# Expert tiles of a two-block transformer: eight raw and six split places for weights instead of four and four

## What is computed

```python
def swiglu(h, wg, wu, wd):
    return (jax.nn.silu(h @ wg) * (h @ wu)) @ wd

def moe_swiglu(h, router, bias, wg, wu, wd):
    logits = (h @ router).astype(jnp.float32) + bias.astype(jnp.float32)
    top_logit, top_idx = lax.top_k(logits, TOP_K)
    ...
    out = jnp.zeros_like(h)
    for e in range(N_EXPERTS):
        out = out + gates[..., e:e + 1] * swiglu(h, wg[e], wu[e], wd[e])
    return out
```

## Time and profile before

| | us |
|---|---|
| median of three executions | 3074.38 (3071.87 to 3077.40) |
| the profiled execution | 3072.45 |
| its span, first to last instruction | 3070.6 |
| first tile of experts to the end | from 2346.4 to 3070.6 |
| of it, six whole tile periods | 2418.3 to 2806.7 |

### The profile page before, as it was taken

The page is one execution under the profiler, slowest core; times in us unless marked ns, Lnnn a source line. Parts: engine busy times, 40 slices in busy tenths (PEclk is TensorE's granted clock), DMA queues, the critical chain, the costliest instruction groups (busy, mean ns, idle before and its releaser), DMA issues.

```text
span 3070.6 us, 54310 instructions
## 1 busy us (share of the span) xinstructions
PE 2717.5 (88%) x21600; PEld 2488.4 (81%) x21600; DVE 2141.7 (70%) x3622; ACT 1384.3 (45%) x2027; POOL 122.4 (4%) x115
## 2 busy tenths in 40 slices
PE   7989899998998998898789998897989988988877
PEld 7878899897888997797779997786888766776655
DVE  6898677588876757674557666755566778777666
ACT  4444444444534444333344443332344565666554
POOL 0000000000000000000000000000000000001454
PEclk9999999999999999898899998997999999999999
DMA  5533445454444553212235542111434777787676
GB/s 193 171 128 133 145 160 193 136 179 153 136 145 138 190 176 108 72 71 70 96 104 175 191 159 96 56 57 63 143 113 146 251 262 251 267 280 264 214 235 209
DMA packets 153738, 485.88 MB, mean 158 GB/s; under 512 B 17136, under 2 KB 27760, under 8 KB 153232
## 3 DMA queue, kind: packets, MB, share of 16 engines
q1 hardware_dynamic: 135664, 424.68, 41.3%
q0 software_dynamic: 13584, 51.91, 5.1%
q10 hardware_dynamic: 4240, 5.81, 0.7%
HBM read 481.29 MB, written 1.05 MB: 157 GB/s over the span
## 4 chain that ended last, share of the span: by engine, by line
PE 56%; DVE 21%; DMA 10%; ACT 7%; issue 6%; POOL 0%; DVEq 0%; ACTq 0%; SPq 0%; POOLq 0%
PE ps L1762 15%; PE ps L1764 14%; PE ps L1763 14%; PE ps L1767 12%; DVE wl L2564 8%; ACT wh L2233 4%; DMA wf<-in_moe_down 3%; DVE b L2576 3%; DVE b L2568 3%; DMA wf<-in_moe_up_a 3%; DMA wf<-in_moe_up_a,b 2%; DVE SC L2576 2%; DVE SC L2568 1%; DMA wf<-in_moe_down,b 1%; DVE RS L2568 1%
## 5 line engine op out<-in xcount | busy, mean ns | idle before, releaser
L2564 DVE TENSOR_TENSOR wl<-wf,wh 128x1024 fp32r<-128x1024 f32 (+3 forms) x934 | 1081.8, 1187 | 354.4 <-ACT wh L2233 349.8
L2233 ACT ACTIVATE wh<-wf 128x1024 fp32r<-128x1024 f32 (+3 forms) x934 | 932.3, 1026 | 462.8 <-PE ps L1764 224.1
L1762 PE MATMUL ps<-b,wh 128*128 128x256 f32 x3096 | 900.5, 291 | 105.5 <-DVE wl L2564 62.2
L1763 PE MATMUL ps<-b,wh 128*128 128x256 f32 x3096 | 888.3, 287 | 0.0
L1764 PE MATMUL ps<-b,wl 128*128 128x256 f32 x3096 | 887.9, 287 | 0.0
L1762 PEld LDWEIGHTS ps<-b,wh 128*128 128x128 f32 x3096 | 607.0, 196 | 119.0 <-issue 88.0
L1763 PEld LDWEIGHTS ps<-b,wh 128*128 128x128 f32 x3096 | 606.9, 196 | 0.2
L1764 PEld LDWEIGHTS ps<-b,wl 128*128 128x128 f32 x3096 | 606.6, 196 | 0.0
L1762 PE MATMUL ps<-wh,b 128*128 128x512 f32 (+2 forms) x748 | 305.8, 409 | 92.6 <-DVE wl L2564 82.1
L1762 PE MATMUL ps<-HH,wh 128*128 128x256 f32 x1264 | 374.0, 296 | 12.7 <-DVE wl L2564 12.6
L1763 PE MATMUL ps<-HL,wh 128*128 128x256 f32 x1264 | 363.8, 288 | 0.0
(11 more groups left out here) (212 smaller groups left out, 2446.3 us busy)
## 6 DMA issues: line engine op xcount, KB each, us to landing
wf<-in_w_in_b SPq DMA_DIRECT2D x112, 512.0 KB, 4.3
wf<-in_moe_up_a SPq DMA_DIRECT2D x112, 512.0 KB, 4.6
wf<-in_w_in SPq DMA_DIRECT2D x80, 512.0 KB, 3.6
wf<-in_moe_down SPq DMA_DIRECT2D x77, 512.0 KB, 4.6
wf<-in_w_ffn_g SPq DMA_DIRECT2D x44, 512.0 KB, 3.6
wf<-in_w_ffn_u SPq DMA_DIRECT2D x44, 512.0 KB, 4.6
wf<-in_moe_up_b SPq DMA_DIRECT2D x56, 384.0 KB, 3.9
wf<-in_w_out SPq DMA_DIRECT2D x32, 512.0 KB, 3.5
```

The source lines that it names most:

```text
L1762: e.matmul(o, stat[0], mov[0], start=first, stop=False)
L1763: e.matmul(o, stat[0], mov[1], start=False, stop=False)
L2233: e.activation(u.whi, u.buf, ACT.Copy).then_inc(u.hi[0])
L2564: e.tensor_tensor(u.wlo, u.buf, u.whi.bitcast(F32), SUB).then_inc(u.lo[0])
```

## The change

Slots are now objects in a ring that can grow: each knows who used it last (`last`), and a unit waits for that instead of the unit four before. Before the first tile four raw slots are added in the arena at 14000 to 18095 (free once the last matmul of `first_up` has read `xg`), so that there are eight. After `add_x0` two pairs of split slots are added at 3584 to 7679 (free once `add_x0` has read `F0`), so that there are six. The tiles' steps split up to four units ahead (`AHEAD_TILE`), all others still two.

```diff
-    SLOT, NRAW, NSPL, AHEAD = 1024, 4, 4, 2
+    SLOT, NRAW, NSPL, AHEAD, AHEAD_TILE = 1024, 4, 4, 2, 4
...
+    class Slots:
+        def __init__(self, views):
+            self.slots, self.i = [], -1
+            self.more(views, None)
+
+        def more(self, views, after):
+            for v in views:
+                a = Step("slot")
+                a.v, a.last = v, after
+                self.slots.append(a)
+
+        def take(self):
+            self.i = (self.i + 1) % len(self.slots)
+            return self.i, self.slots[self.i]
+
+    def used_by(hi, lo, free):
+        a = Step("use")
+        a.hi, a.lo, a.free = hi, lo, free
+        return a
+
+    raws, splits = Slots(WF), Slots(list(zip(WH, WL)))
...
-        u.z, u.f = u.i % NSPL, u.i % NRAW
+        f, raw = raws.take()
+        _, split = splits.take()
+        u.raw_after, u.split_after, raw.last, split.last = raw.last, split.last, u, u
...
+                if read is not None:
+                    read[:] = [st.bk.full]
...
-            st.split_to = u.i + 1 + AHEAD
+            st.split_to = u.i + 1 + AHEAD_TILE
...
-        fd0 = yield from first_up(ins["moe_wg_2"], ins["moe_wu_2"], 11, F0, ADDED, routing)
+        x_read = []
+        fd0 = yield from first_up(ins["moe_wg_2"], ins["moe_wu_2"], 11, F0, ADDED, routing, x_read)
...
+        raws.more([big(14000 + SLOT * i, SLOT) for i in range(4)], used_by(x_read, None, None))
...
+                splits.more([[big(3584 + 2 * SLOT * i + SLOT * z, SLOT, dt=F32R) for z in range(2)] for i in range(2)], used_by(None, None, end0))
...
-                if u.i >= NSPL:
-                    E.wait_ge(units[u.i - NSPL].free)
+                if u.split_after is not None:
+                    E.wait_ge(u.split_after.free)
...
-                E.wait_ge(units[u.i - NRAW].hi)
-                E.wait_ge(units[u.i - NRAW].lo)
+                E.wait_ge(u.raw_after.hi)
+                E.wait_ge(u.raw_after.lo)
```

More of the change, by code:

```diff
@@ L288, in unit_of @@
         u.i = len(units)
-        u.z, u.f = u.i % NSPL, u.i % NRAW
         u.src, u.m, u.n, u.rows = src, m, n, rows
-        u.raw = P.next(f"w_raw{u.f}" if rows is None else f"w_rows{u.f}", 16)
+        f, raw = raws.take()
+        _, split = splits.take()
+        u.raw_after, u.split_after, raw.last, split.last = raw.last, split.last, u, u
+        u.raw = P.next(f"w_raw{f}" if rows is None else f"w_rows{f}", 16)
         u.hi = P.next("w_hi")
@@ L295, in unit_of @@
         w = u.m * u.n
-        u.buf, u.whi, u.wlo = WF[u.f][:, 0:w], WH[u.z][:, 0:w], WL[u.z][:, 0:w]
+        u.buf = raw.v[:, 0:w]
+        u.whi, u.wlo = [x[:, 0:w] for x in split.v]
         units.append(u)
@@ L963, in block1_mix, with first_up @@
         residual_rms(Y, yd, 0.5, ys)
-    def first_up(Wg, Wu, nt, F2, parts, side=None):
+    def first_up(Wg, Wu, nt, F2, parts, side=None, read=None):
         fd, late = {}, []
@@ L3311, in sp_program @@
                 continue
-            if u.i >= NRAW:
-                E.wait_ge(units[u.i - NRAW].hi)
-                E.wait_ge(units[u.i - NRAW].lo)
+            if u.raw_after is not None:
+                E.wait_ge(u.raw_after.hi)
+                E.wait_ge(u.raw_after.lo)
             e.dma_start(u.buf.rearrange("p (m n) -> p m n", n=u.n), u.src).then_inc(u.raw[0], 16)
```

## The result

The median fell from 3073.7 us (four executions) to **2955.3 us** (2950.21 to 2962.21), a ratio of 0.9615 with a 95% interval of 0.9592 to 0.9637. The span of the profiled execution is 2951.6 us, 119.0 less than before.

The account below looks back on a forecast made before the run. The prediction took a latency loop of too few raw slots as the bound. SP periods −49, start +5 and POOL tiles −39 summed to −83 us, giving 2991 us, with a range of 2958 to 3025.

Parts of the forecast that it names:

- The latency loop: Tiles: four raw slots, each reused after 6.8 to 7.3 us, bind; eight allow a unit per 0.9, even 1.3 us.
- 53.6 + 2 + 1 = 56.5 us: SP tile period: TensorE floor, later banks at the scatter, first matmuls starting behind a wait; six periods save 49 us.
- +8: Start: first new raw slot waits for the last first-expert gemm, so the third unit is ready 8 us later.
- +2: Start: new split slots wait for the first expert's last matmul behind the additions, costing 2 us.
- −3: Start: splitting four ahead covers part of VectorE's overflow work in the first tile, saving 3 us.
- −2: Start: the first tile's own waits for transfers go, saving 2 us.
- (35 − R) × 1.25 us: POOL tiles: least break time for loads with R low-part runs per 35 units; R = 16 gave 65 us a period.
- POOL is not held: Rival, POOL tiles: the 105 units also go at 1.61 us each, saving 64 us; 2966 us in all, chance 0.20.
- Long runs starve POOL: Rival, POOL tiles: ten low-part runs, 72 us a period, saving only 17 us; 3013 us in all, chance 0.20.
- rows 12: Earlier trace, POOL tiles: one load of 2.72 us ending 0.82 after four back-to-back low parts; read as loads being held.
- The wait moves to the banks: Rival: two extra splits cost more steps than the scatter; SP periods 60 us, 3021 us in all, chance 0.12.
- Slower: Rival: transfers at their limit at 268 GB/s, more slots only lengthen landings; +30 us, 3104 in all, chance 0.04.

Follow-up runs that it names:

- e1: Changed kernel with eight raw slots, but only four split places and two units ahead: 2971.1 us, 0.9685 of the kernel before.
- e2: Changed kernel with only four raw slots, keeping six split places and four units ahead: 3072.1 us, 1.0006 of the kernel before.
- e10: Changed kernel with eight raw slots and four units ahead, but without the two added split places: 2975.1 us, 0.9696.
- e5: Changed kernel with both rings beginning again at their first old place when they grow: 2939.3 us, 0.9579.
- e9: Kernel of e5 (old places first) with two more raw slots, ten in all: 2934.3 us, 0.9565.
- e7: Changed kernel with splits two instead of four units ahead in the three overflow tiles: 2955.7 us, 0.9633.
- e11: Kernel of e5 (old places first) with splits three units ahead in the overflow tiles: 2943.3 us, 0.9594.
- e6: Changed kernel with overflow tiles loading fixed experts' weights by SP's plain loads instead of POOL's indirect ones: 2943.2 us, 0.9595.
- e12: Changed kernel with the overflow tiles' low part made as raw unit times zero, one SBUF input instead of two: 2938.9 us, 0.9586.

## Why the prediction missed

The direction, the cause and the start were right; the size was 36 us short in the span, in two steps: 14 us in the SP periods and 20 in the POOL tiles (the rest, 2 us, lies ahead of the first tile).

**The latency loop: right.** Slots alone give 97 us, the rest alone nothing (e1, e2), and ScalarE's wait for transfers is gone. That 1.3 us a unit would be enough was borne out down to six slots.

**The SP period: mis-sized.** "53.6 + 2 + 1 = 56.5 us" measured 54.1, 14 us over six periods. The floor of TensorE was right to 0.5. The 2 us at the scatter are not there: the wait is 0.40 us, where it was 0.48. I let VectorE arrive late at the gate step. But its 49.8 us of work in 54.1 leave it ahead, so the two extra splits are done before TensorE ends the step and delay nothing. They cost a wait of 1.94 us when the places are missing (e10). The 1 us for starts behind a wait fell away with the waits: the period opened at 2585.10 has no other gap of TensorE over 0.1 us.

**The start: right.** "+8", "+2", "−3" and "−2" made +5, measured +5.5. The third unit starts 5.3 us later than before by the time of the span, 7 counted from the earlier gemm end, for the 8 expected. Behind the additions TensorE waits 2.1 and 1.0 us where it waited 3.6 once: −0.5 for "+2" and "−3". That leaves −1 for the "−2".

**The POOL tiles: the step that failed.** "A POOL load does not get through while low parts follow each other without a gap" was read from one load. VectorE and POOL of the changed kernel, in order of time:

```profile
2815.91 2.35 DVE L2597 TENSOR_TENSOR wl<-b,wh 128x1024 fp32r<-128x1024 f32 x2
2818.19 1.22 DVE L2597 TENSOR_TENSOR wl<-wf,wh 128x1024 fp32r<-128x1024 f32 x1
...
2817.11 1.97 POOL L3331 DMA_INDIRECT b<-in_moe_down,b  x1 [0.30 <-issue]
2819.39 0.94 POOL L3331 DMA_INDIRECT b<-in_moe_down,b  x1 [0.31 <-issue]
```

The low part under which the load starts ends at 2818.26 and the next begins at 2818.19, with no gap. The load ends at 2819.08, 0.82 us behind the first, while the second still runs. In the changed kernel 49 loads start under a low part that another follows within 0.06 us. Of them 46 are over within 0.95 us of the first one's end; three (2.3 to 2.7 us long) are held to the end of the next as well. So a run without gaps as a rule lets a load through every 1.97 + 0.30 = 2.27 us, not one in all. The load of the earlier trace rows was one of the exceptions, and the trace before had the rule: 21 of 24. Longer exceptions exist, 4.0 us in e5 and e9, 4.7 in e7, 7.9 in e11. What decides between the two cases no run here shows. Two groups of the line's loads (count, duration ns min/median/max):

```profile
L3331 POOL DMA_INDIRECT b<-in_moe_up_a,b x24: 933/946/2662, 2740.3 to 2897.8; - x24
...
L3331 POOL DMA_INDIRECT wf<-in_moe_down,b x17: 933/1054/1968, 2811.8 to 2928.4; - x17
```

With R runs the formula asked for (35 − R) × 1.25 us of breaks. The changed kernel has 13 and 19 runs in two overflow periods (12 and 14 when breaks under 0.06 us are not counted), for which it gives 68 and 61 us or more; both last 58. The forecast of 65 was 7 us a tile too long, 20 in all. The average load takes 1.26 us and 0.30 go between: 35 of them are **54.7 us**, just above TensorE's 54.1. Raw units come late, the gate step stands behind them, and TensorE waits 2.7 and 3.0 us for it; the stretch at half clock behind each wait makes up the 58 (e7). The forecast had no term for the clock, though it was 0.95 in these tiles before. e9 and e6 agree: more slots change nothing in sum, plain loads give 54.2.

**The rivals.** "POOL is not held" (2966; first in the list, though the working calls it the second) was nearest, though its mechanism is wrong: loads are held, but the queue costs some 10 us where I had priced the hold at 25. "Long runs starve POOL" fell with the reading of rows 12. "The wait moves to the banks" is true in the overflow tiles alone (2.7 us), and there it comes with late raw units. "Slower" fell: 319 GB/s over 270 us, though landings grew to 8.3 us at the longest, over the 7 I had named. The Trainium skill (SBUF — State Buffer, Who interferes with whom) infers that a tensor-tensor operation leaves descriptor writing alone, but has it contend with what GpSimd reads from SBUF when both its inputs lie there. The prediction took the first half alone. The loads here read their row numbers from SBUF and are held, 1.97 us in place of 0.94; that agrees with the second half, and which access is held no run shows. The time that the first half would have given (2966) was nearer than mine. The section also lists tensor-scalar among the operations that can take the shared ports; e12 agrees, with 1.33 us behind one of 0.69.

## What to carry to other kernels

When a wait for transfers shows in a chain that returns to the same buffer, divide that loop by the number of buffers and compare with the next bound; the smallest number that falls well under it is enough (here six where five were not). The average is not all: with five the loop gave 51 us a period and the late units still made TensorE wait. An added lead costs nothing while the engine that makes it arrives early, so compare its work with the period before pricing the delay. Where a wait of TensorE is taken away or made, look at the granted clock behind it: here waits of 1.9 to 3.2 us were most often followed by 3.4 us at half the clock, another 1.7 us. And a rule of contention read from a single instruction is worth checking on all its kind: a hundred loads were in the trace.

## What was not expected of the hardware

A POOL indirect load ends 0.82 us after the VectorE operation under which it starts, most often also if another follows at once (46 of 49 in the changed kernel): 1.97 us at worst in these cases, 0.94 undisturbed. A few are held through a whole run of operations, 7.88 us in one case (e11). It is so with a multiplication by a constant, one input from SBUF, as well (1.33 us, e12), and that operation took 0.69 us for 1024 columns where the subtraction took 1.22. Eight transfers in flight raised the median landing of the up weights from 4.7 to 5.5 us (longest 6.4 and 8.3) over the SP periods, while the rate rose from 268 to 319 GB/s.
